# A channel projection by Strassen's seven block products in place of eight

## The reference

```python
h = rms_norm(x, norm1_gain)                 # (2048 tokens, 1024)
proj = h @ w_in                             # 1024 x 3232 columns
sb = proj[..., :1536]                       # q, k, v of the stick-breaking heads
rw = proj[..., 1536:]                       # 1696 channels of the RWKV-7 heads
pf = rw + (previous_token(rw) - rw) * mu    # token shift
# q, k -> rms_norm; stick-breaking attention; RWKV-7 recurrence on pf;
# x += mix @ w_out; x += top-2 of 32 SwiGLU experts
```

## Time and profile before

| | us |
|---|---|
| median of 3 runs | 2692.89 (2690.38 to 2694.44) |
| the profiled execution | 2691.94 |
| its span, first to last instruction | 2690.1 |
| TensorE busy in it | 2513.9 |
| VectorE busy | 1237.1 |
| ScalarE busy | 1060.0 |
| GpSimd busy | 811.9 |

### The profile page before, as it was taken

The page is one execution under the profiler, slowest core; times in us unless marked ns, Lnnn a source line. Parts: engine busy times, 40 slices in busy tenths (PEclk is TensorE's granted clock), DMA queues, the critical chain, the costliest instruction groups (busy, mean ns, idle before and its releaser), DMA issues. The chain is left out here.

```text
span 2690.1 us, 87465 instructions
## 1 busy us (share of the span) xinstructions
PE 2513.9 (93%) x36952; PEld 1590.9 (59%) x36953; DVE 1237.1 (46%) x2508; ACT 1060.0 (39%) x2120; POOL 811.9 (30%) x944
## 2 busy tenths in 40 slices
PE   7999999999999999688888888998799999999998
PEld 3444444444467777477777764555466567666676
DVE  2333312121299999467667645666422222222222
ACT  1111110000077778666666633444133333333333
POOL 0000031000000000456666623332344444444443
PEclk9999999999999999899999999998799999999999
DMA  4111131111122203011111104643599988889993
GB/s 146 59 58 58 58 106 70 47 70 47 51 85 76 71 15 111 25 35 50 47 42 48 45 14 159 203 129 137 180 320 326 324 302 293 306 300 375 301 323 87
DMA packets 227333, 370.10 MB, mean 138 GB/s; under 512 B 35009, under 2 KB 116417, under 8 KB 224418
## 3 DMA queue, kind: packets, MB, share of 16 engines
q1 hardware_dynamic: 213186, 328.72, 35.4%
q0 software_dynamic: 13920, 38.03, 5.9%
HBM read 296.17 MB, written 70.52 MB: 136 GB/s over the span
## 5 line engine op out<-in xcount | busy, mean ns | idle before, releaser
L2511 PE MATMUL gu_ps<-gate_up_,xT 128*32 128x256 f32 x6336 | 362.3, 379 | 7.6 <-issue 6.5
L347 PE MATMUL ps<-low,high 128*128 128x512 f32 x768 | 336.9, 595 | 2.5 <-issue 2.5
L2588 DVE STREAM_TRANSPOSE xT<-xg 128x256 f32<-128x256 f32 x145 | 95.2, 657 | 471.8 <-PE gu_ps L2511 468.3
L2511 PEld LDWEIGHTS gu_ps<-gate_up_,xT 128*32 128x32 f32 x6336 | 219.2, 110 | 133.6 <-DVE h L2602 25.3
L2566 ACT COPY y<-y_ps 32x256 f32<-32x256 f32 x576 | 209.6, 364 | 190.3 <-PE y_ps L2520 181.1
L2520 PE MATMUL y_ps<-down_,hT 128*32 128x256 f32 x4608 | 278.6, 379 | 1.7 <-ACT y L2566 1.7
L347 PEld LDWEIGHTS ps<-low,high 128*128 128x128 f32 x768 | 144.3, 191 | 173.0 <-issue 173.0
L722 DVE TENSOR_TENSOR_SCAN h_all<-h_all 128x512 f32<-128x512 f32 x192 | 243.0, 1326 | 2.6 <-ACT h_all L680 2.3
L2479 POOL DMA_INDIRECT out<-y,put x144 | 194.4, 1350 | 155.5 <-issue 91.5
L2471 POOL DMA_INDIRECT xg<-h,take x146 | 144.6, 991 | 291.5 <-DVE h L2602 267.1
L2520 PEld LDWEIGHTS y_ps<-down_,hT 128*32 128x32 f32 x4608 | 166.5, 110 | 85.2 <-ACT y L2566 2.2
(11 more groups left out here) (352 smaller groups left out, 4627.5 us busy)
## 6 DMA issues: line engine op xcount, KB each, us to landing
down_<-in_w_exp_down SPq DMA_DIRECT2D x128, 512.0 KB
gate_up_<-in_w_exp_gate SPq DMA_DIRECT2D x88, 512.0 KB
gate_up_<-in_w_exp_up SPq DMA_DIRECT2D x88, 512.0 KB
high<-in_w_exp_gate SPq DMA_DIRECT2D x40, 512.0 KB
high<-in_w_exp_up SPq DMA_DIRECT2D x40, 512.0 KB
pT<-low SPq DMA_DIRECT2D x13, 1024.0 KB, 3.9
rkv<-pT SPq DMA_DIRECT2D x96, 128.0 KB, 2.5
high<-in_x SPq DMA_DIRECT2D x16, 512.0 KB, 4.0
```

The costliest lines, as they stand in the source:

```text
L347: done = pe.matmul(qkv_ps[:, part, :], hT[:, s, k, :], w_sb[:, k, part * SBW:(part + 1) * SBW], start=(k == 0), stop=(k == KT - 1))
L2511: last = pe.matmul(gu_ps[QUARTERS[q], 0:2 * P].rearrange("t (x f) -> t x f", x=2), xT[:, k * ROWS:(k + 1) * ROWS], w_gu[s][:, k, :, q * P: ...
L2588: dve.transpose(xT[:, :].rearrange("p (k t) -> p k t", k=KT), xg[j][:, :].rearrange("t (p k) -> t k p", k=KT))
```

## The change

The chunks 0 to 11 are taken in six pairs. With the two chunks of a pair as rows, the two halves of k as the inner dimension, and the two halves of the tokens as columns, each pair is a 2 by 2 block product, made by Strassen's scheme (in Winograd's form) from seven products. Sums of h blocks (T1 to T4) are made once, sums of weight blocks (S1, S2, S4 and one in place) for each pair, all by VectorE, which also adds the products into `p_raw`. Chunk 12 runs first, in the old way. The first pair of heads is loaded near the end of the stage, `no_key` is made after the rest, `shifted` is one buffer, and the loops are written out. Cut to its core:

```diff
-    shifted = front.low[:, 0:2 * SEQ].rearrange("p (s t) -> p s t", t=SEQ)
+    T1, T2, T3, T4 = [rows_of(t) for t in (low[:, 0:2 * SEQ], high[:, 0:2 * SEQ], high[:, 2 * SEQ:4 * SEQ], rkv_flat[:, 0:2 * SEQ])]
+    shifted = low[:, AT:AT + SEQ]
+    last_shifted = low[:, BLOCK * 2:BLOCK * 2 + SEQ]
...
     def on_sync(sp):
         sp.wait_ge(front.projected, NT * 3)
-        load(sp, 1, 1)
+        load(sp, 0)
         sp.wait_ge(front.stored, CREDIT + NT * 48)
         sp.wait_ge(front.edged, 16)
         sp.wait_ge(front.h_kept, 2 + NT)
-        load_first_pair(sp)
+        load(sp, 1)
+        store(SINGLE, 1, shifted)
+        for p in range(CHUNK_PAIRS):
+            if p == CHUNK_PAIRS - 1:
+                sp.wait_ge(projected, made_of(p, 1, 4))
+                load_first_pair(sp)
+            for a in range(2):
+                store(2 * p + a, mixed_of(p, a), last_shifted if p == CHUNK_PAIRS - 1 and a == 1 else shifted)
+            if p + 2 < CHUNK_PAIRS:
+                load(sp, p + 2)
...
     def on_tensor(pe, last_turn):
+        def block_products(to, w, h):
+            for k in range(KT // 2):
+                done = pe.matmul(to, w[:, k, :], h[:, k, :], start=(k == 0), stop=(k == KT // 2 - 1))
+            return done
...
+        def seven(p, j):
...
+            if p >= 1:
+                pe.wait_ge(taken, taken_of(p - 1, j, 4))
...
+            block_products(bank(j, BANK_A), w_block(p, 0, 0), h_block(0, 0, j)).then_inc(projected, 1)
+            pe.wait_ge(summed, sums_of(p, 2))
+            if p >= 1:
+                pe.wait_ge(taken, taken_of(p - 1, j, 5))
+            block_products(bank(j, BANK_B), S2, columns(T2, j)).then_inc(projected, 1)
+            block_products(bank(j, BANK_C), S1, columns(T1, j)).then_inc(projected, 1)
+            pe.wait_ge(summed, sums_of(p, 3))
+            if p >= 1:
+                pe.wait_ge(taken, taken_of(p - 1, j, 6))
+            block_products(bank(j, BANK_D), w_block(p, 1, 0), columns(T3, j)).then_inc(projected, 1)
+            pe.wait_ge(copied, copied_of(p, j))
+            block_products(bank(j, BANK_A), w_block(p, 0, 1), h_block(1, 0, j)).then_inc(projected, 1)
+            pe.wait_ge(summed, sums_of(p, 4))
+            pe.wait_ge(taken, taken_of(p, j, 1))
+            block_products(bank(j, BANK_B), S4, h_block(1, 1, j)).then_inc(projected, 1)
+            pe.wait_ge(taken, taken_of(p, j, 2))
+            block_products(bank(j, BANK_D), w_block(p, 1, 1), columns(T4, j)).then_inc(projected, 1)
...
+        for p in range(CHUNK_PAIRS):
+            act.wait_ge(mixed, mixed_of(p - 1, 0) if p else 1)
+            for j in range(2):
+                act.wait_ge(projected, made_of(p, j, 1))
+                act.copy(p_raw[:, 0, 1 + j * GT:1 + (j + 1) * GT], bank(j, BANK_A)).then_inc(copied, 1)
...
     def on_gpsimd(pool):
         pool.wait_ge(front.projected, NT * 3)
+        rec.make_masks(pool)
+        pool.wait_ge(projected, front.ALL_MADE)
         pool.memset(front.no_key, 0.0)
...
-        rec.make_masks(pool)
...
     def on_vector(dve):
+        def sum_w(p, last):
+            first, second = [[w_block(p, a, half) for half in range(2)] for a in range(2)]
+            if last:
+                dve.tensor_tensor(S4, first[1], S2, ALU.subtract).then_inc(summed, 1)
+                return
+            dve.wait_ge(w_loaded[p % 2], p // 2 * 64 + 64)
+            dve.tensor_tensor(S1, second[0], second[1], ALU.add).then_inc(summed, 1)
+            dve.drain()
+            dve.tensor_tensor(S2, S1, first[0], ALU.subtract).then_inc(summed, 1)
+            dve.tensor_tensor(second[0], first[0], second[0], ALU.subtract).then_inc(summed, 1)
+            dve.drain()
...
+        def put_together(p, j):
+            to11, to12, to21, to22 = [place(a, cols, j) for a in range(2) for cols in range(2)]
+            dve.wait_ge(copied, copied_of(p, j))
+            dve.wait_ge(projected, made_of(p, j, 2))
+            dve.tensor_tensor(to12, to11, bank(j, BANK_B), ALU.add).then_inc(taken, 1)
+            dve.drain()
+            dve.wait_ge(projected, made_of(p, j, 4))
+            dve.tensor_tensor(to21, to12, bank(j, BANK_D), ALU.add).then_inc(taken, 1)
+            dve.tensor_tensor(to12, to12, bank(j, BANK_C), ALU.add)
+            dve.drain()
+            dve.tensor_tensor(to22, to21, bank(j, BANK_C), ALU.add).then_inc(taken, 1)
+            if j == 1 and p + 1 < CHUNK_PAIRS:
+                sum_w(p + 1, False)
+            dve.wait_ge(projected, made_of(p, j, 5))
+            dve.tensor_tensor(to11, to11, bank(j, BANK_A), ALU.add).then_inc(taken, 1)
+            dve.wait_ge(projected, made_of(p, j, 6))
+            dve.tensor_tensor(to12, to12, bank(j, BANK_B), ALU.add).then_inc(taken, 1)
+            if j == 1 and p + 1 < CHUNK_PAIRS:
+                sum_w(p + 1, True)
+            dve.wait_ge(projected, made_of(p, j, 7))
+            dve.tensor_tensor(to21, to21, bank(j, BANK_D), ALU.add).then_inc(taken, 1)
+            dve.drain()
+
+        def mix_tokens(c, a, to, stores):
+            if stores:
+                dve.wait_ge(stored, stores * 16)
+            dve.tensor_tensor(to, p_raw[:, a, 0:SEQ], p_raw[:, a, 1:1 + SEQ], ALU.subtract)
+            dve.drain()
+            dve.scalar_tensor_tensor(to, to, mu[:, c:c + 1], p_raw[:, a, 1:1 + SEQ], ALU.mult, ALU.add).then_inc(mixed, 1)
+
...
+        dve.tensor_tensor(T1, whole[0][1], whole[0][0], ALU.subtract).then_inc(summed, 1)
+        dve.wait_ge(front.stored, CREDIT + NT * 48)
+        dve.tensor_tensor(T3, whole[1][1], whole[0][1], ALU.subtract).then_inc(summed, 1)
+        dve.drain()
+        dve.tensor_tensor(T2, whole[1][1], T1, ALU.subtract).then_inc(summed, 1)
+        dve.drain()
+        dve.tensor_tensor(T4, whole[1][0], T2, ALU.subtract).then_inc(summed, 1)
+        dve.wait_ge(mu_loaded, FIRST_LOADED)
+        dve.wait_ge(projected, NG)
+        sum_w(0, False)
+        sum_w(0, True)
+        dve.wait_ge(copied, NG)
+        mix_tokens(SINGLE, 0, shifted, 0)
+        for p in range(CHUNK_PAIRS):
+            for j in range(2):
+                put_together(p, j)
+            last = p == CHUNK_PAIRS - 1
+            mix_tokens(2 * p, 0, shifted, 2 * p + 1)
+            mix_tokens(2 * p + 1, 1, last_shifted if last else shifted, 0 if last else 2 * p + 2)
```

More of the change, by code:

```diff
@@ new lines, in project_channels @@
+    raw = [[low[:, AT + SEQ + x * BLOCK:AT + SEQ + (x + 1) * BLOCK] for x in range(3)] + [fourth[:, :]],
+           [high[:, 4 * SEQ + x * BLOCK:4 * SEQ + (x + 1) * BLOCK] for x in range(4)]]
+    w_first = front.w_first
+    first_flat = w_first[:, :, :].rearrange("p k c -> p (k c)")
+    S1, S2, S4 = [block_of(t) for t in (first_flat[:, 0:BLOCK], first_flat[:, BLOCK:2 * BLOCK], rkv_flat[:, 2 * SEQ:2 * SEQ + BLOCK])]
+    w_rest = raw[0][0][:, 0:KT * REST].rearrange("p (k c) -> p k c", c=REST)
@@ L388, in project_channels, with w_block, bank, h_block @@
-    NCH = NFULL + 1
-    give_credit(nc, mixed, copied)
+    taken, mixed = front.channels_taken, sem("p2_mixed")
+    summed = sem("p2_summed")
+    BANK_A, BANK_B, BANK_C, BANK_D = range(4)
+    def w_block(p, a, half):
+        return block_of(raw[p % 2][2 * a + half])
+    def bank(j, which):
+        return p_ps[:, 4 * (1 - j) + which, :]
+    def h_block(half, cols, j):
+        return h_all[:, half * 4:half * 4 + 4, cols * HALF + j * GT:cols * HALF + (j + 1) * GT]
+    def made_of(p, j, n):
+        return NG + 14 * p + 7 * j + n
@@ L431, in on_tensor @@
     def on_tensor(pe, last_turn):
[L432 to L443, removed]
-                else:
-                    pe.wait_ge(copied, CREDIT + c * NG - 2 * NG + g + 1)
-                for k in range(KT):
-                    last = pe.matmul(p_ps[:, s, g, :], w[s][:, k, :], h_all[:, k, g * GT:(g + 1) * GT],
-                                     start=(k == 0), stop=(k == KT - 1))
-                last.then_inc(projected, 1)
@@ new lines, in on_tensor @@
+        pe.wait_ge(mu_loaded, FIRST_LOADED)
+        for g in range(NG):
+            if g == 0:
+                pe.wait_ge(front.h_kept, 2 + NT)
+            if g == 1:
+                last_turn(pe)
+            if g == 2:
+                pe.wait_ge(front.qkv_copied, CREDIT + NT * 3)
+            for k in range(KT):
+                last = pe.matmul(p_ps[:, g, :], w_first[:, k, :], h_all[:, k, g * GT:(g + 1) * GT], start=(k == 0), stop=(k == KT - 1))
+            last.then_inc(projected, 1)
@@ L508, in on_vector @@
-        with dve.Fori(0, LOOPED // 2) as i:
-            for s in range(2):
-                chunk(i * 2 + s, s, i)
-        for c in range(LOOPED, NFULL):
-            chunk(c, c % 2, c // 2)
+        def sum_w(p, last):
[9 more added lines that the diff above has]
+            dve.drain()
```

167 lines of the change are left out of this document (86 added, 81 removed).

## The result

The changed kernel takes 2643.85 us (median of 4 runs, 2637.86 to 2644.95), the kernel before, beside it, 2691.64 (4 runs, 2688.41 to 2694.44). The ratio is 0.9817, with an interval of 0.9803 to 0.9831: the change takes off 47.8 us, by the interval 45.5 to 53.0. All ratios in this document leave out two executions that took far longer than all others: 3281.58 us of the kernel before, beside `before_moved`, and 5488.8 us of `after_met`.

What follows compares the result with a forecast made beforehand. TensorE's work was taken to bound the channel projection, with serial work behind it. Matmuls -41.2 us and the end +5.3 give -35.9, so the median of 2692.89 becomes 2657 us, range 2650 to 2670.

Steps and rivals of the forecast that it cites:

- The matmuls: Channel projection: six pairs take 672 records in place of 768, so TensorE loses 41.2 us of work.
- Boundaries at 0: Channel projection: 84 products in place of 48 groups, each with its own waits, cost TensorE 0 us.
- VectorE in a pair: Channel projection: VectorE's adds, weight sums and mixes, 22 us per pair beside 48 of TensorE, leave the pairs gapless.
- the slack of 1.9 us: Boundary between pairs: VectorE's first add ends 1.9 us before TensorE's sixth product wants it.
- the third rival: Pair boundaries: the single `shifted` buffer waits for late stores and stalls TensorE; 2671 us (chance 0.07) or 2698.5 (0.03).
- The start: Beside the odd chunk, run first: VectorE makes T1 to T4 (4.45 us each) and two weight sums; slack 1.8 us, cost 0.
- The end: From the last projection matmul to VectorE's first scan: 14.8 us in place of 9.5, costing 5.3 us.
- E: The time when the last projection matmul ends: 731.8 us in the kernel before, forecast 690.6 after.
- the lock: Behind the projection: GpSimd's difference of v and VectorE's two-SBUF-input instructions exclude each other, adding 4.2 to 4.3 us.
- the second rival: Behind the projection: VectorE is stopped and TensorE's clock falls with it, so the tail costs twice; 2660 to 2663 us, chance 0.18.
- the last clause of the first part: Said of the attention behind the channel projection, where VectorE's scans set the pace: what comes after is serial behind it.
- what the sum says: Whole kernel: -41.2 us for the matmuls and +5.3 for the end give -35.9 us.

Runs made afterwards that it cites:

- before_moved: Kernel before with 128 semaphore increments ahead of TensorE's first transposes: 2692.4 us, ratio 0.9994.
- after_met: Changed kernel with 49 small matmuls (196 instructions) ahead of TensorE's first transposes: 2658.13 us, ratio 0.9857 to the kernel before.
- mix_longer: Changed kernel with the subtraction of the even chunk's mix made three times in pairs 0 to 4: 2667.93 us, ratio 0.9885 to the kernel before.
- The repeated ones: Kernel before with 48 matmuls added, one repeated ahead of each group of chunks 1 to 12: 2729.33 us, ratio 1.0121.
- before_hidden: Kernel before with 32 small matmuls (128 instructions) ahead of TensorE's first transposes, where TensorE waits anyway: 2680.6 us, ratio 0.9945.

## Why the prediction was right, and where it was wrong

- *The matmuls.* 48 matmuls, 96 records at 0.4293 us, 41.2 us: stood. 672 records of L492 in 288.94 us, against 288.5, so the twelve chunks take 40.8 us less. The repeated ones gave them back: first scan 40.8 us later for 48.
- *Boundaries at 0.* Stood. One wait of 0.20 us in 84 products.
- *VectorE in a pair, the slack of 1.9 us.* Stood: `mix_longer` shows the chain, and 1.9 again. Of the third rival, the stalls in the pairs, nothing came: the store ahead of the odd chunk's mix landed in 3.9 us.
- *The start.* The sums T1 to T4 took 4.42 us each, against 4.45; the second weight sum ended at 403.7, as forecast, 1.7 us ahead of its use.
- *The end.* First scan forecast at E + 14.8, measured at E + 10.2, for the lock fell on one of the eight scans and not ahead of them; their end was forecast at the same time either way. With it the end costs 5.0 us, against 5.3. Of the second rival the mechanism came and its price did not: TensorE had the lower granted level, 0.50, from 706.1 to 712.9, but VectorE sets the pace there, and the attention was no longer for it (348.6 against 349.5). The loads of v did not show. Here the Trainium skill's rule on the shared port ("SBUF — State Buffer", Who interferes with whom) agrees with the trace: the first scan took 4.72 us beside GpSimd's difference, and 0.42 in the kernel before.
- *The step that failed* is the last clause of the first part: "What comes after it is serial behind it." I took from it that the 1950 us behind the first scan keep their length. They are serial, but their length hangs on something that the change does move: how many instructions TensorE has taken before them, and so where its fetches fall between the stores. In its place the runs showed a time behind the first scan that was 12 to 13 us shorter, of which the late stores account for 9.1 and 7.6 us in the two pairs of traces. None of my rivals had it, and of what could make the prediction wrong I named the length of the attention alone, where nothing happened. The trace of the kernel before does hold the sign of it: two stores of even tiles landed in 5.4 us beside others in 3.6, and the routing stage had pairs of 33.1 us beside others of 30 to 31. I did not read that stage.

The Trainium skill ("Runtime: NRT & Kernel Launch", Instruction fetch mechanics) says that the instruction memory is refilled in blocks of 16 KiB and that crossing a boundary is "mostly hidden". The packet size agrees with the trace. That it is hidden agrees too, for TensorE: in the stretch of the changed kernel above it was busy for 213.17 of 213.20 us, with six fetches in it. For a store on another queue, of which the page says nothing there, it was not: it lost 1.7 to 2.2 us.

With the placement alike, the change is worth what the sum says, as far as these runs can tell. Both with the short stage: 2648.7 against 2680.6 of `before_hidden`, 31.9 us, or by the two ratios 49.3 - 14.8 = 34.5. Both with the long one: `after_met`, 38.5 off, 40.9 without its later start. The forecast of 35.9 lies between them; each of these differences is uncertain by some 7 us, by the two intervals that it is made of.

Open are three things. The remaining 3 to 6 us of the surplus: the timed medians have them, and so do the controls without any of the change. Behind the first scan `before_hidden` won 15 us and `before_moved` 12, and the routing stage with the stretch ahead of it accounts for some 10 in either. So that part too may hang on the instruction count, but nothing shows how: the recurrence varies between 454.9 and 467.4 us in these traces, with both extremes in kernels of the changed code, and hides any cause of that size. Why the fetch delays the store: the packet is one of 286 in its window and takes 1.2% of the engines' time, so it is not its bytes; no experiment looked inside the queue. And a version that has the change and a placement chosen well on purpose: the changed kernel as it stands has at most one late store, so there is no more than about 2 us to be had in this stage.

## What to carry to other kernels

A saving on the engine that bounds a stage pays one for one where the next stages are serial behind it, and the price lies in what is moved to the stage's end: here a GpSimd operation that had been beside matmuls and then stood beside scans. When a change alters the number of instructions ahead of a loop whose pitch is close to the pitch of the instruction fetches, some of the difference may have nothing to do with the change (here 12 to 15 us, about 0.5%), so time a control that has the old work and the new count. A stretch that gets faster without having been touched is a reason to compare the DMA landings in it, one by one, before the engines.

## What the runs showed of the hardware

- Stores of 512 KB with a 16 KB instruction fetch 0.7 to 3.2 us behind their issue landed in 5.2 to 5.7 us (12 of 12 even tiles); with no fetch within 3.8 us behind, 3.6 us (69 of 69).
- 128 instructions of useless work, put where TensorE waits, made the kernel 0.55% faster.
- 128 semaphore increments at TensorE's start moved its first transpose from 11.34 to 23.44 us. If they begin where the small matmuls of `before_hidden` do, at 3.80, they take 0.15 us each, an estimate.
- Behind five waits of 2.5 us each in a stage of matmuls, the product took 5.4 and 5.3 us at two boundaries and 3.7 at three; the granted clock was 0.81 over the 9 us around the first and 1.00 around the second, as the two stops of the earlier trace rows had differed. A fall cost 1.6 to 1.8 us more.
- One GpSimd operation of 6.5 us held a scan of VectorE up by 4.3 us; with that operation on VectorE, for 2.3 us, the eight scans were back at 5.82 from 10.13.
- A stretch of 460 us, the recurrence, differed by 11.5 us between two executions of the same kernel (454.9 and 466.4).
